# A loop on TensorE in place of three written-out pairs of expert rounds

## The reference, cut to what matters

```
def moe_ffn(h, router, w_gu, w_down):
    logits = (h @ router).astype(jnp.float32)
    top_v, top_i = lax.top_k(logits, TOP_K)
    w = jax.nn.softmax(top_v, axis=-1)
    combine = jnp.sum(jax.nn.one_hot(top_i, N_EXPERTS, dtype=jnp.float32) * w[..., None], axis=-2)
    gu = jnp.einsum('btd,edf->btef', h, w_gu)
    g, u = jnp.split(gu, 2, axis=-1)
    act = jax.nn.silu(g) * u * combine[..., None].astype(h.dtype)
    return jnp.einsum('btef,efd->btd', act, w_down)
```

## Time and profile before

| | |
|---|---|
| time, median of 3 runs | 2413.27 us (2411.2 to 2414.54) |
| profiled execution, its own time | 2411.2 us |
| its span, first to last instruction | 2409.4 us |
| TensorE busy | 2251.9 us, 93% |
| VectorE, ScalarE busy | 474.7 us, 394.8 us |
| mean granted TensorE clock | 0.973 |
| DMA traffic | 551.95 MB, mean 229 GB/s |
| code packets of TensorE's own queue (q8) | 155, 2.54 MB |
| expert rounds of layer 1, of layer 3 | about 805 to 1185 us, 2006 to 2386 us |

### The profile page before, as it was taken

One profiled execution on the slowest core, in us unless ns is written; L12 is line 12 of the kernel. 1 busy time (PEld: TensorE's weight loads), 2 busy tenths in 40 slices (PEclk: granted clock), 3 DMA queues, 4 the chain that ended last, 5 costly groups with the idle time before them and its releaser, 6 DMA issues.

```text
span 2409.4 us, 44071 instructions
## 1 busy us (share of the span) xinstructions
PE 2251.9 (93%) x19623; PEld 1620.0 (67%) x19623; DVE 474.7 (20%) x1337; ACT 394.8 (16%) x819; POOL 67.3 (3%) x111
## 2 busy tenths in 40 slices
PE   7999998999998999999798899999989889999996
PEld 4776667888887545445476588888878875444354
DVE  2235332000112200000111410002345332000001
ACT  1133223000101000000113310002143321000000
POOL 4000001000000000000000000000000000000000
PEclk8999999999999999999899899999999989999999
DMA  8967889653355699999474695413430067999981
GB/s 321 286 236 265 320 308 276 193 157 105 104 179 181 216 388 381 379 386 327 166 224 169 221 284 161 131 53 105 141 122 7 13 226 246 386 380 379 387 311 44
DMA packets 356292, 551.95 MB, mean 229 GB/s; under 512 B 11408, under 2 KB 311312, under 8 KB 343616
## 3 DMA queue, kind: packets, MB, share of 16 engines
q1 hardware_dynamic: 344352, 525.31, 62.7%
q0 software_dynamic: 5840, 18.11, 3.0%
q10 hardware_dynamic: 5920, 5.78, 0.7%
HBM read 537.64 MB, written 15.98 MB: 230 GB/s over the span
## 4 chain that ended last, share of the span: by engine, by line
PE 87%; DVE 5%; DMA 3%; ACT 3%; issue 1%; SPq 0%; ACTq 0%; POOL 0%; DVEq 0%; POOLq 0%
PE ps L641 85%; DMA ring<-in_moe_w_down 2%; ACT ring L1402 1%; ACT work L1402 1%; DVE ring L1967 0%; DVE ring L1949 0%; DMA work<-y_rows,work 0%; DVE work L1808 0%; SPq L476 0%; DVE ring L1972 0%; DVE ring L1957 0%; PE ps L1032 0%; DMA ring<-in_ada_w 0%; PE ps L1139 0%; DVE xT L2339 0%
## 5 line engine op out<-in xcount | busy, mean ns | idle before, releaser
L641 PE MATMUL ps<-ring,work 128*32 128x384 f32 (+6 forms) x7752 | 696.8, 449 | 44.9 <-ACT work L1402 24.9
L641 PE MATMUL ps<-hT,ring 128*128 128x256 f32 x3200 | 712.6, 382 | 2.7 <-DVE hT L1818 2.5
L641 PEld LDWEIGHTS ps<-hT,ring 128*128 128x128 f32 x3200 | 607.9, 191 | 112.1 <-issue 11.6
L641 PEld LDWEIGHTS ps<-ring,work 128*32 128x32 f32 (+2 forms) x7752 | 335.0, 115 | 385.0 <-issue 252.6
L1402 ACT ACTIVATE work<-ps 128x256 f32<-128x256 f32 (+5 forms) x244 | 103.7, 438 | 1364.9 <-PE ps L641 1198.2
L641 PE MATMUL ps<-work,ring 128*128 128x256 f32 (+1 forms) x1344 | 291.0, 376 | 10.5 <-DVE work L2034 6.0
L641 PEld LDWEIGHTS ps<-work,ring 128*128 128x128 f32 (+1 forms) x1344 | 243.9, 189 | 48.1 <-DVE work L2034 8.4
L641 PE MATMUL ps<-ring 64*64 64x64 f32 (+1 forms) x4192 | 182.7, 229 | 17.5 <-ACT ring L1402 7.2
L641 PEld LDWEIGHTS ps<-ring 64*64 64x64 f32 x4192 | 160.4, 138 | 56.4 <-ACT ring L1402 24.2
L1402 ACT ACTIVATE ring<-ps 128x512 f32<-128x512 f32 (+3 forms) x208 | 101.6, 491 | 339.9 <-PE ps L641 328.9
L641 PE MATMUL ps<-work 128*128 128x128 f32 (+1 forms) x768 | 104.5, 290 | 4.7 <-DVE work L2154 4.6
(11 more groups left out here) (258 smaller groups left out, 971.3 us busy)
## 6 DMA issues: line engine op xcount, KB each, us to landing
ring<-in_moe_w_gu SPq DMA_DIRECT2D x96, 1536.0 KB, 15.7
ring<-in_ada_w SPq DMA_DIRECT2D x96, 1024.0 KB, 6.9
ring<-in_moe_w_down SPq DMA_DIRECT2D x48, 1536.0 KB, 16.3
ring<-in_ff_w_gu SPq DMA_DIRECT2D x88, 512.0 KB, 5.9
ring<-in_dn_w_in SPq DMA_DIRECT2D x32, 1024.0 KB, 5.5
ring<-in_moe_w_gu SPq DMA_DIRECT2D x32, 1024.0 KB, 8.4
ring<-in_ff_w_down SPq DMA_DIRECT2D x44, 512.0 KB, 7.0
ring<-in_moe_w_down SPq DMA_DIRECT2D x32, 512.0 KB, 11.3
```

The source lines that it names most:

```text
L641: return pe.matmul(out, lhsT, rhs, start=start, stop=stop, **kw)
```

## The change

TensorE's three written-out pairs of rounds become a loop of its sequencer with three turns; `r` is a register in it, in both layers.

```
@@ -1305,7 +1305,7 @@
                 gather(0)
                 gather(1)
                 body(q0, True)
-                for r in range(1, NARROW, 2):
+                with pe.Fori(1, NARROW, 2) as r:
                     small(q0 + r)
                     body(q0 + r + 1, False)
                 pe.wait_ge(moe["d_np"], i + 1)
```

## The result

| | before | after |
|---|---|---|
| time, median | 2413.35 us (4 runs, 2411.2 to 2414.54) | 2441.11 us (4 runs, 2435.23 to 2444.99) |
| profiled execution, own time | 2411.2 us | 2439.59 us |
| span | 2409.4 us | 2437.8 us |
| ratio, 95% interval | | 1.0114 (1.0091 to 1.0137) |

It is 24 to 28 us slower; forecast were 7.3, with 2431 us as the upper end of the range.

What follows compares the result with a forecast made beforehand. Expert stages run at DMA's pace until each layer's second weight wait, then at TensorE's. Four jumps x (3.8 stall + 2.1 clock) = 23.6, minus 12.1 waits and 4.2 clock losses, gives +7.3 us: 2420.6, range 2411 to 2431.

Steps and rivals of the forecast that it cites:

- What bounds the stage: Expert stages of layers 1 and 3: DMA pace until the second weight wait, then TensorE's; lateness is first paid from waits.
- Register arithmetic and branch at nothing: TensorE's loop in layers 1 and 3: hidden behind queued matmuls, taken as 0; without that cover branches cost 0.3 us.
- no stall: At the jumps back: code packet still held, four branches give 2413.6 us at most; shares chance 0.29 with the absorbed case.
- No jump back in the trace, so the fetch had to be bounded: At each jump back, TensorE's code fetch estimated at 5.4 us, ends 2.2 and 7.2, from small transfers in the same traffic.
- S: TensorE's stall at each jump back: 5.4 us fetch less 1.6 us sequencer lead, 3.8 us; ends 0.6 and 5.6, or 0.
- The packet behind the first: After a jump back, the code packet behind the first may also come late; no size given.
- The clock: After each stalled jump TensorE drops to 1.2 GHz, losing 2.1 us a jump, ends 0 and 2.5.
- The sum: Layers 1 and 3: jumps 23.6 us, minus 12.1 of weight waits and 4.2 of clock losses, +7.3 us.
- much slower: At the jumps, stall plus clock loss 8.1 us: +16.1, 2429.4 us; DMA dry some 2 us past 14 us lateness, 2431; chance 0.17.
- signs of being wrong: In the profile after: no idle at the jumps, idle under 3 us, stalls in more places, or GB/s dipping behind the second jump.
- Faster: At the jumps, a 3.0 us stall just fills the weight waits and keeps the clock: -4.2 us, 2409.1; chance 0.07.
- Absorbed: At the weight waits behind the jumps: a 2.5 us stall with the clock kept leaves nothing, 2413.3 us; chance 0.29 including held code.

Runs made afterwards that it cites:

- 6th kernel: The change with its loop turning twice and the third pair written out, one jump a layer: 2417.79 us against 2413.76, ratio 1.0017.
- 4th: The change's loop in both layers plus an instruction at its head naming the end branch and its target: 2410.06 us against 2412.91, ratio 0.9990.
- 10th: The 4th kernel once more, unchanged, beside the kernel before on another chip: 2411.16 us against 2413.02, ratio 0.9983.
- 7th: Kernel before plus five matmul loops, 1000 to 2240 instructions a turn, quiet traffic: all nine jumps up to 1760 take 0.2 us, above 3.3 to 3.9.
- 8th: The change with work left out of the bodies, one turn 1549 instructions instead of 2173: four jumps 0.2 us each; total time says nothing.
- 5th kernel: The change with the loop's first instruction placed on the first place of a code packet: 2431.24 us against 2413.76, ratio 1.0079.

## Why the prediction was wrong

**What bounds the stage**: right. Waits for weights at the bodies took up lateness (6th kernel), and all four went.

**Register arithmetic and branch at nothing**: right. The 4th and 10th kernels have all the registers and jumps and are not slower; a branch that is not taken lasts 67 to 88 ns. A taken one with its target held lasts 0.2 us (7th and 8th kernels), so four of them would be 0.8 us and not the 0.3 of the "no stall" rival.

**No jump back in the trace, so the fetch had to be bounded**: the mechanism was right (4th, 7th and 8th kernels), the size not. The forecast took 5.4 us for the fetch and 1.6 us of lead. The branch lasts 6.2 to 6.5 us, and the lead is 1.4 us: branch at 935.9, idle from 937.26 us. A third term was missing: from the branch's end to the first matmul another 0.5 us pass (942.23 to 942.76). The idle is 5.3 to 5.6 us, mean 5.44, for S = 3.8. The rows nearest to it were transfers of another engine's queue, 5.8 and 7.2 us, and I took a value under both. The 1.1 us of a packet is the small part of the stall: 3.7 to 3.9 us pass before it starts, and 1.4 us after it has landed. Four jumps x 1.64 = 6.6 us.

**The packet behind the first**: here a step was missing. It stood only as half a sentence in the "much slower" rival, unpriced. In layer 1 the loop's head has four matmuls left in its packet, so TensorE stood again, 3.72 + 3.93 = 7.65 us. The 5th kernel shows the cause, and the code queue fits it: the next packet starts only at 945.55 us, 3.3 us after the branch has ended, and TensorE goes on 2.4 us later, at 947.97.

**The clock**: right in size. The matmuls from the jump to the next turn take 1.50 + 21.53, 1.50 + 22.43, 22.98 and 22.45 us, and 20.83 us in the 10th kernel, where the clock stays up. So c is 2.2, 3.1, 2.2 and 1.6 us, mean 2.3 for 2.1.

**The sum**, with the measured terms: 4 x (5.44 + 2.3) + 7.65 - 12.1 - 4.2 = 22.3 us, against the 22.1 of the two chains. So its form held, and two terms failed: S (+6.6) and the missing second idle (+7.65). The medians' 24 to 28 us leave 2 to 6 more; the repeated timing, at 24.2, takes away most. That the last 2 us are variation, or a cost of the loops outside the pairs, is not shown.

**The rivals**: "much slower" had the right sign and named the second packet, but its end of 2431 us was short, since it priced only the first. Its dry queue came, already behind the first jump of layer 1 at some 9 us of lateness instead of over 14, and cost nothing instead of 2 us. Of the prediction's own signs of being wrong two came: idles in more places than the four jumps, and GB/s that dip. "Faster" did not happen in the change, but its mechanism did in layer 1 of the 10th kernel, at idles of at most 2 us instead of some 3. "Absorbed" was wrong by the size of S.

## What to carry to other kernels

Before a written-out stretch becomes a loop, count the engine's instructions in one turn, an fp32 matmul as four: here TensorE jumped for 0.2 us up to 1760 and stalled at 2000. A longer turn wants a hint, or each jump costs a fetch, 3.3 to 3.9 us in quiet traffic and 6.3 in full, and a second one if the head stands near the end of a packet. And subtract the waits behind a stall before adding it up: one jump a layer cost 4 us where two cost 24.

## What I had not expected of the hardware

A jump to code that is not held ends 2.3 to 2.7 us after its code packet has started, with a hint or without, in quiet traffic or full; a hint only moves that start. So a hinted jump is not free (1.1 to 2.7 us of branch), and moving the loop's head to a packet's start does not shorten it. A short idle ahead of a longer wait can gain time: idles of 1.5 and 2.0 us at the jumps cut the waits for weights from 1.9 and 4.1 us to one of 1.8, and saved the 2.5 us that TensorE had lost at 1.2 GHz.

But how long an idle is does not settle what the clock does. Behind idles of about 2.3 us it fell once (6th kernel, layer 3) and stayed up once (kernel before, layer 3).
